# One core, two decoder blocks: the mixer's head norms, gates and last cell step placed in the memory stage, and output products that wait for the split parts one at a time

## What is computed

```python
go = rmsnorm(go.transpose(0, 2, 1, 3), gdn_norm_w) * jax.nn.silu(g_z...)
...
h = num / jnp.maximum(jnp.abs(den), jnp.exp(-m_t))[..., None]
...
mh = rmsnorm(mh.transpose(0, 2, 1, 3), mlstm_norm_w...) * jax.nn.sigmoid(m_o...)
mixed = jnp.concatenate([go..., mh...], axis=-1)
return mixed @ w_out
```

## Time and profile before

| | us |
|---|---|
| median of 3 runs | 2404.67 |
| lowest and highest | 2404.33, 2405.97 |
| span of the profiled execution | 2405.3 |
| PE busy in it | 2268.6 |
| DVE busy | 1544.9 |
| ACT busy | 1126.1 |
| POOL busy | 51.6 |

### The profile page before, as it was taken

How to read it: one execution, slowest core, us unless ns; L and a number is a source line. 1 busy time by engine, 2 the same in 40 slices (tenths; PEclk the granted TensorE clock), 3 DMA queues, 4 the chain that set the end, 5 groups by cost and what they waited for, 6 DMA issues and landing times. The chain is left out here.

```text
span 2405.3 us, 38363 instructions
## 1 busy us (share of the span) xinstructions
PE 2268.6 (94%) x15466; PEld 2086.1 (87%) x15466; DVE 1544.9 (64%) x2713; ACT 1126.1 (47%) x1961; POOL 51.6 (2%) x26
## 2 busy tenths in 40 slices
PE   8979888999999999999999999999999999988998
PEld 8867676999999997888878998979998899867997
DVE  7866445999888985666655456665456545575554
ACT  5523334455554445555555344444443434474443
POOL 0121000100000000000000000000000000000000
PEclk9989889999999999999999999999999999889999
DMA  6362233355444445666646555535555655303552
GB/s 260 139 67 91 88 129 127 120 178 182 158 142 148 144 147 177 193 195 194 195 127 251 182 187 211 193 134 215 191 178 192 228 183 186 125 19 123 197 188 105
DMA packets 78310, 390.25 MB, mean 162 GB/s; under 512 B 9772, under 2 KB 12716, under 8 KB 49741
## 3 DMA queue, kind: packets, MB, share of 16 engines
q1 hardware_dynamic: 76684, 383.59, 46.3%
q0 software_dynamic: 1040, 4.19, 1.6%
q10 hardware_dynamic: 432, 0.33, 0.0%
HBM read 382.83 MB, written 5.24 MB: 161 GB/s over the span
## 5 line engine op out<-in xcount | busy, mean ns | idle before, releaser
L246 DVE TENSOR_TENSOR split_slots<-ring,split_slots 128x1024 fp32r<-128x1024 f32 x406 | 481.9, 1232 | 333.7 <-ACT split_slots L237 333.6
L339 PE MATMUL banks<-x_transposed_hi,split_slots 128*128 128x256 f32 x1920 | 549.8, 286 | 8.8 <-DVE split_slots L246 5.2
L340 PE MATMUL banks<-x_transposed_lo,split_slots 128*128 128x256 f32 x1920 | 547.9, 285 | 0.0
L341 PE MATMUL banks<-x_transposed_hi,split_slots 128*128 128x256 f32 x1920 | 547.6, 285 | 0.0
L237 ACT ACTIVATE split_slots<-ring 128x1024 fp32r<-128x1024 f32 x406 | 404.4, 1049 | 222.6 <-PE banks L341 197.2
L350 DVE SCALAR_TENSOR_TENSOR expert_lo<-ring,expert_hi 128x512 fp32r<-128x512 f32 x512 | 363.2, 714 | 173.8 <-ACT expert_hi L345 172.7
L345 ACT ACTIVATE expert_hi<-ring 128x512 fp32r<-128x512 f32 x512 | 323.2, 632 | 266.8 <-PE banks L341 266.7
L339 PEld LDWEIGHTS banks<-x_transposed_hi,split_slots 128*128 128x128 f32 x1920 | 372.2, 194 | 11.5 <-DVE split_slots L246 5.6
L340 PEld LDWEIGHTS banks<-x_transposed_lo,split_slots 128*128 128x128 f32 x1920 | 372.1, 194 | 1.5
L341 PEld LDWEIGHTS banks<-x_transposed_hi,split_slots 128*128 128x128 f32 x1920 | 372.1, 194 | 0.0
L339 PE MATMUL banks<-x_transposed_hi,expert_hi 128*128 128x256 f32 x1024 | 296.8, 290 | 5.5 <-DVE expert_lo L350 5.5
(11 more groups left out here) (463 smaller groups left out, 3431.8 us busy)
## 6 DMA issues: line engine op xcount, KB each, us to landing
ring<-in_ffn_w SPq DMA_DIRECT2D x132, 1024.0 KB, 4.8
ring<-in_peer_u SPq DMA_DIRECT2D x128, 512.0 KB, 3.5
ring<-in_peer_v SPq DMA_DIRECT2D x128, 512.0 KB, 4.3
ring<-in_w_in SPq DMA_DIRECT2D x16, 1024.0 KB, 5.1
ring<-in_sgu_w_in SPq DMA_DIRECT2D x16, 1024.0 KB, 4.8
ring<-in_peer_wq SPq DMA_DIRECT2D x8, 1024.0 KB, 5.0
ring<-in_sgu_w_out SPq DMA_DIRECT2D x8, 1024.0 KB, 4.8
ring<-in_kv_w SPq DMA_DIRECT2D x6, 1024.0 KB, 4.8
```

The costliest lines, as they stand in the source:

```text
L246: ins = dve.tensor_tensor(self.parts[:, b, 1, p], self.k.w.slot(g)[:, p], self.parts[:, b, 0, p].bitcast(F32), ALU.subtract)
L339: pe.matmul(out, lh, rh, start=start, stop=False)
L340: pe.matmul(out, lh, rl, start=False, stop=False)
L341: return pe.matmul(out, ll, rh, start=False, stop=stop)
```

## The change

In the memory stage PE runs `memory_cell(3)` between the two halves of panel 6. ACT and DVE get the head norms and the gates there: squares, sums, roots, inverses, and the multiplications by scale and gate, in place in `s.go` and `s.mh`; the division by the denominators is there too. The mixer's output stage keeps the transposes (straight from `s.go` and `s.mh`, into banks 4 to 7), both halves of `Beginning`, and the splits of the four banks. `attend_memory` mixes into banks 4 to 7 as well. The output products don't wait for all parts at their head; before each tile of a slot PE waits for the count of written parts that the tile needs (`Before.part`). The tile `mixed` is gone.

```diff
@@ -296,8 +296,10 @@
 class Before:
 
 
-    def __init__(self, splits_eaten, highed=None, written=None, banks_read=()):
+    def __init__(self, splits_eaten, highed=None, written=None, banks_read=(), parts=None):
         self.splits_eaten, self.highed, self.written, self.banks_read = splits_eaten, highed, written, banks_read
+        self.parts = parts
+        self.waited = 0
 
     def rows_high(self, pe):
         for signal, value in self.banks_read:
@@ -308,6 +310,16 @@
     def rows_low(self, pe):
         if self.written:
             pe.wait_ge(*self.written)
+
+    def part(self, pe, m, i):
+
+        if m == 0 and i == 0:
+            for signal, value in self.banks_read:
+                pe.wait_ge(signal, value)
+        value = self.parts(m, i)
+        if value > self.waited:
+            self.waited = value
+            pe.wait_ge(self.written[0], value)
 
 
 def high_first(pe, before, out, operands, x_on_right):
...
@@ -1349,7 +1361,10 @@
         gain = k.sb(ctx, "head_gains", [P, HD + GW])
         vs, ps, acts, pools, landed, gained, panel_done, panel_read = (k.sig.new() for _ in range(8))
         ws, outs, dstate, mouts, mdstate, vns, decayed, gds, mds, rd, mrd = (k.sig.new() for _ in range(11))
-        A_, MAXD, MPREV, MNEXT, INTER, MT, SCARG, WARG, R, WGT = range(10)
+        head_squared, head_summed, head_rooted, head_inverted, head_scaled, divided = (k.sig.new() for _ in range(6))
+        A_, MAXD, MPREV, MNEXT, INTER, MT, SCARG, WARG, R, WGT, DEN = range(11)
+        SUMS, ROOTS, SCALES = 11, 13, 15
+        read, squares, gates = (s.go, s.mh), (diag, work), (s.z, s.mo)
         gl = s.glast[:, 0, :].rearrange("p (h n) -> p h n", h=HEADS)
         dec = s.glast[:, 1, :].rearrange("p (h n) -> p h n", h=HEADS)
 
@@ -1473,10 +1488,10 @@
             panel(5, 1)
             memory_cell(2)
             panel(6, 0)
+            memory_cell(3)
             panel(6, 1)
             panel(7, 0)
             panel(7, 1)
-            memory_cell(3)
 
         @block.vector
         def _(dve):
@@ -1594,6 +1609,43 @@
             low(7)
             mlstm_add(2)
 
+            def head_sums(n):
+                dve.wait_ge(head_squared, n + 1)
+                dve.tensor_reduce(c[:, SUMS + n, :], squares[n][:, :, :], AX_X, ALU.add).then_inc(head_summed, 1)
+
+            def scale_and_gate(n):
+                dve.wait_ge(head_rooted, n + 1)
+                dve.reciprocal(c[:, SCALES + n, :], c[:, ROOTS + n, :]).then_inc(head_inverted, 1)
+                dve.wait_ge(head_inverted, n + 1)
+                dve.wait_ge(gained, n + 1)
+                for i in range(TILES):
+                    own = read[n][:, i, :, :]
+                    dve.tensor_tensor(own, own, over_last(c[:, SCALES + n, HEADS * i:HEADS * i + HEADS], HD), ALU.mult
+                                      ).then_inc(head_scaled, 1)
+                    dve.wait_ge(head_scaled, TILES * n + i + 1)
+                    dve.tensor_tensor(own, own, gates[n][:, i, :].rearrange("p (h d) -> p h d", h=HEADS), ALU.mult)
+
+            def divide():
+                dve.wait_ge(mrd, NCHUNK)
+                by_tile = c[:, DEN, :].rearrange("p (i h) -> p i h", h=HEADS)
+                dve.scalar_tensor_tensor(by_tile, s.mden[:, :, :, 0], -1.0, s.mden[:, :, :, 0], ALU.mult, ALU.max
+                                         ).then_inc(divided, 1)
+                dve.wait_ge(divided, 1)
+                dve.tensor_tensor(by_tile, by_tile, s.emt[:, :].rearrange("p (h i) -> p i h", h=HEADS), ALU.max
+                                  ).then_inc(divided, 1)
+                dve.wait_ge(divided, 2)
+                dve.reciprocal(c[:, DEN, :], c[:, DEN, :]).then_inc(divided, 1)
+                dve.wait_ge(divided, 3)
+                dve.tensor_tensor(s.mh[:, :, :, :], s.mh[:, :, :, :],
+                                  over_last(c[:, DEN, :], HD).rearrange("p (i h) d -> p i h d", h=HEADS), ALU.mult
+                                  ).then_inc(divided, 1)
+
+            head_sums(0)
+            scale_and_gate(0)
+            divide()
+            head_sums(1)
+            scale_and_gate(1)
+
         @block.scalar
         def _(act):
             def delta_out(n):
@@ -1640,9 +1692,27 @@
             copy(5)
             split.high(act, 7)
             cell_out(2)
+
+            def head_squares(n):
+                act.activation(squares[n][:, :, :].rearrange("p (i h) d -> p i h d", h=HEADS), read[n][:, :, :, :], ACT.Square
+                               ).then_inc(head_squared, 1)
+
+            def head_roots(n):
+                act.wait_ge(head_summed, n + 1)
+                act.activation(c[:, ROOTS + n, :], c[:, SUMS + n, :], ACT.Sqrt, bias=k.eps[:, 0:1], scale=1.0 / HD
+                               ).then_inc(head_rooted, 1)
+
+            act.wait_ge(rd, NCHUNK)
+            act.wait_ge(ps, 3)
+            head_squares(0)
+            head_roots(0)
+            cell_out(3)
+            act.wait_ge(vs, 33)
+            act.wait_ge(divided, 4)
+            head_squares(1)
             copy(6)
+            head_roots(1)
             copy(7)
-            cell_out(3)
 
         @block.gpsimd
         def _(pool):
...
-        highs, lows = split_turned(k, 0, dst, banks, high, written)
+        highs, lows = split_turned(k, 4, dst, banks, high, written)
...
@@ -1687,46 +1745,24 @@
 
         @block.scalar
         def _(act):
-            act.activation(sq_g, s.go[:, :, :, :], ACT.Square).then_inc(acts, 1)
-            begin.high(act, 0)
-            act.wait_ge(vs, 4)
-            act.activation(sq_m, heads(mo), ACT.Square).then_inc(acts, 1)
-            act.wait_ge(vs, 6)
-            act.activation(c[:, 2, :], c[:, 1, :], ACT.Sqrt, bias=k.eps[:, 0:1], scale=1.0 / HD).then_inc(acts, 1)
-            begin.high(act, 1)
+            begin.highs(act)
             highs(act)
 
         @block.vector
         def _(dve):
-            link = linker(dve, vs)
-            d = c[:, 0, 0:8].rearrange("p (i h) -> p i h", h=HEADS)
-            link(dve.scalar_tensor_tensor(d, s.mden[:, :, :, 0], -1.0, s.mden[:, :, :, 0], ALU.mult, ALU.max))
-            link(dve.tensor_tensor(d, d, s.emt[:, :].rearrange("p (h i) -> p i h", h=HEADS), ALU.max))
-            link(dve.reciprocal(c[:, 0, 0:8], c[:, 0, 0:8]))
-            link(dve.tensor_tensor(heads(mo), src_m, per_head(c[:, 0, 0:8]), ALU.mult))
-            dve.wait_ge(acts, 1)
-            link(dve.tensor_reduce(c[:, 1, 0:8], sq[:, 0:8, :], AX_X, ALU.add))
-            begin.low(dve, 0)
-            dve.wait_ge(acts, 2)
-            link(dve.tensor_reduce(c[:, 1, 8:16], sq[:, 8:16, :], AX_X, ALU.add))
-            dve.wait_ge(acts, 3)
-            link(dve.reciprocal(c[:, 3, :], c[:, 2, :]))
-            for i in range(TILES):
-                for n, (src, out, gate) in enumerate(((s.go, go, s.z), (heads(mo), mo, s.mo))):
-                    own = heads(out)[:, i, :, :]
-                    scale = over_last(c[:, 3, 8 * n + 4 * i:8 * n + 4 * i + 4], HD)
-                    link(dve.tensor_tensor(own, src[:, i, :, :], scale, ALU.mult))
-                    dve.tensor_tensor(out[:, i, :], out[:, i, :], gate[:, i, :], ALU.mult).then_inc(normed, 1)
-            begin.low(dve, 1)
+            begin.lows(dve)
             lows(dve)
 
         @block.tensor
         def _(pe):
             for i in range(TILES):
-                turn_chunks(pe, k, mixed[:, i, :], i, banks, 0, normed)
+                for n, heads in enumerate((s.go, s.mh)):
+                    for h in range(HEADS):
+                        ins = pe.transpose(k.psum[:, 4 + 2 * i + n, h * P:(h + 1) * P], heads[:, i, h, :], k.ident[:, :])
+                    ins.then_inc(banks, 1)
 
         k.idle_pool(block)
-        k.before = Before((written, 4), (high, 4), (written, 4))
+        k.before = Before((written, 4), (high, 4), (written, 4), parts=lambda m, i: 2 * i + m // 2 + 1)
     return gains_landed, 32
 
 
...
@@ -1796,7 +1832,7 @@
         c = k.sb(ctx, "xa_columns", [P, 4, PAIRS])
         scored, maxed, negated, expd, recip, scaled, turned, copied, mixed, high, written = (k.sig.new() for _ in range(11))
 
-        highs, lows = split_banks(k, 0, k.xT, mixed, high, written)
+        highs, lows = split_banks(k, 4, k.xT, mixed, high, written)
         begin, before = Beginning(k), k.before
 
         @block.sync
@@ -1825,7 +1861,7 @@
                 for half in range(2):
                     for m in range(2):
                         lo = h * DH + half * P
-                        ins = pe.matmul(k.psum[:, h, half * SEQ:(half + 1) * SEQ], v[:, m, lo:lo + P],
+                        ins = pe.matmul(k.psum[:, 4 + h, half * SEQ:(half + 1) * SEQ], v[:, m, lo:lo + P],
                                         probT[:, h, m, :], start=(m == 0), stop=(m == 1))
                 ins.then_inc(mixed, 1)
 
@@ -1860,7 +1896,7 @@
             highs(act)
 
         k.idle_pool(block)
-        k.before = Before((written, 4), (high, 4), (written, 4))
```

(15 more changed lines are left out.)

14 lines of the change are left out of this document (1 added, 13 removed).

## The result

The changed kernel takes 2385.7 us (median of 4 runs, 2384.55 to 2390.2), the kernel before 2404.5 beside it: 18.8 us faster. The ratio is 0.9924, with a 95% interval from 0.9912 to 0.9937, which is 15 to 21 us. The forecast was 2389.0, 15.7 us faster. The profiled execution of the changed kernel is the one that took 2390.2 us, the highest of its four, with a span of 2388.4; against the profiled span of before that is 16.9 us. A run's time is 1.8 to 1.9 us longer than the span of the same execution. So the profiled execution of before, with its span of 2405.3, took about 2407.1 and lies some 2.5 us above its median, and not between the lowest and the highest run; that of the changed kernel lies 4.5 above its own. The difference is why the two spans show 16.9 and the medians 18.8.

A forecast was written before the change was run, and what follows sets the result against it. PE was taken to bound the kernel, busy 2268.6 of 2405.3 us; 11.3 + 1.9 + 1.4 + 1.1 = 15.7 us gave span 2389.6, and with the median 0.6 below it, 2389.0. Range 2385.5 to 2394.

The forecast's parts named there:

- The memory stage: Moved cell and head work fit beside PE's last panels: cost 0, DVE ending at 283.3 with 1 us to spare.
- The seam: Between memory stage and mixer's output products: PE starts its products at 288.7 instead of 299.96, 11.3 us sooner.
- The clock: The 96 products behind the mixer run at full clock, 22.47 us instead of 24.39: 1.9 us won.
- a fall in the seam: Rival: the clock falls ahead of the mixer's output products, gain 13.8 us, 2390.9; chance 0.25, including the skill's rule.
- The rival from the Trainium skill's rule: Transposes don't count as busy time, so the clock is gone at the mixer's output: 2390.9; chance 0.05 of the 0.25.
- The two attentions: PE's waits before output products shrink: 1.4 us won behind the cross attention, 1.1 behind the sparse attention.
- the waits by parts bring nothing: Rival: at both attentions another wait takes their place, gain 13.2 us, 2391.5; chance 0.08.
- the chain doesn't fit: Rival: DVE's moved chain outlasts the panels and holds the memory stage's end, 2390.5 to 2393; chance 0.12.
- the head work runs late: Rival: memory-stage head work runs behind PE's last product, costing 7.6 us, 2396.6, or 2402.2 if delta is late; chance 0.05.
- the cell stalls PE: Rival: the last cell stalls PE in panel 6 because DVE's state comes late; 2409 with 20 us; chance 0.02.
- each later stop of PE meets the clock in another phase: Behind the change, each stop may move up to 1.9 us either way; 3 us allowed in the sum.

The follow-up runs named there:

- three kernels with delays: Changed kernel with 14, 22 or 34 more products ending PE's memory-stage work, about 1.0, 2.0 and 3.4 us of delay: 2388.13, 2390.21 and 2388.48 us.
- whole waits: Changed kernel, but PE waits for all written parts in front of each of the three output products, as before: 2396.13 us.
- the long transposes: Changed kernel with 80 more transposes behind the sixteen of the mixer's output stage: 2390.91 us in one run.
- the second median: The changed kernel measured again with no edit: 2385.33 us, 5 runs, ratio 0.9920.
- the run with the longer chain: Changed kernel with three more sums, results not used, in DVE's chain for the mLSTM half: 2389.59 us in one run.

## Why the prediction was right

It was right in direction, size and mechanism, 3 us short in the total, and the reason that it gave for the clock in the seam was too weak.

**The memory stage.** DVE's chain was put at 283.3 with 1 us to spare before the stage's end. It ended at 284.07 in an execution that was 0.6 late, 283.5, with 0.9 to spare. The stage's end was to be unmoved; it came 0.15 later. That the cell's wait costs nothing held. DVE was not busy all the time, as I had said it would be: it waits 1.22 us for the last cell, 1.19 for ACT's squares and twice 0.37 for a root.

**The seam.** 11.3 was forecast, 30.71 - 19.59 = 11.1 measured; the missing 0.15 is the stage's end. Slot 1 was to be ready 0.4 us ahead of PE. The first two of DVE's six low parts from 292.27 are slot 1's; at 6.91 us for six they were ready at 292.27 + 2.3 = 294.6, and PE was through slot 0, a quarter of the 22.48, at 289.44 + 5.6 = 295.0.

**The clock.** 1.9 was forecast, 24.39 - 22.48 = 1.91 measured. The rival, a fall in the seam, did not come in either trace of the changed kernel. The reason that was given does not carry this, though. The prediction counted the clock as kept because each gap was shorter than the 2.7 us in which it had fallen; with gaps of 0.30 and 2.24 us, no longer than those of the changed kernel, it fell in two of the three kernels with delays, for 1.5 and 1.4 us. With whole waits and 4.03 us idle it fell too. So the term was right and in part lucky, and the chance of 0.25 for a fall was not too high. The rival from the Trainium skill's rule fell with the long transposes.

**The two attentions.** 1.4 and 1.1 were forecast; both waits, 1.46 and 1.15, are gone.

**The rivals.** That the waits by parts bring nothing is refuted by the run without them. That the chain doesn't fit, that the head work runs late and that the cell stalls PE are refuted by the rows: panels 6 and 7 follow the cell without a gap. The run with the cell last gives the price that "late head work" would have had, 7.5 us for my sum of 7.6, and the clock with it, which that rival left out.

**What was off.** The total. The places of the change hold 15.7 us, and the medians 18.6 to 18.8. At 2385.7 us the result lies 0.2 inside the low end of the range, 2385.5, and the second median, 2385.33, lies 0.2 outside it. The step that was too small is "each later stop of PE meets the clock in another phase": I took it as noise around the sum, 3 us either way. Over 129 runs of all kernels of this study (each less the mean of its kernel) the time goes with the mean granted clock, -1.2 us for each 0.001 of clock, with a correlation of -0.73. The changed kernel's runs have 0.970, those of before 0.965 in the middle. In the traces the changed kernel has fewer stretches at a lowered clock: that at 890 us is at full clock in both executions, those at 1255 and 1450 in the second alone. In these traces, then, what lies beyond the sum is clock. That it is so for the medians is likely and not shown, since the one trace of the kernel before is not of an execution at its median. And that the shift of 13 to 16 us brings it, and would bring it again, is not shown at all. The delayed kernels show in their rows that the clock at one stop can be there or gone after a pure shift, for 1.5 us; what sets it at the stops far behind stays open.

## What to carry to other kernels

Work that runs alone at a stage's end may be done beside the last products if the step that feeds it is put one place earlier in PE's list; add up the chain on the other engines behind that step and compare it with what PE still has to do, and the difference is the spare time. A wait in front of products should name the part that the first product reads: it is worth its own length, and more where the shorter idle time keeps the clock up. Read a change of some us off the rows at its own places, not off the total: 1.1 us that were plain in the rows did not show in five runs, and the clock at stops far behind moved the total by 4.

## What the runs showed of the hardware

- Ahead of the mixer's output products PE stands still twice, with 1.94 us of transposes between. With 0.94 and 2.24 us the clock stayed full in both traces of the changed kernel; with 0.30 and 2.24 it fell in two kernels of three; with 0.94 and 1.10 it stayed, with 0.94 and 4.03 it fell, and so it did with 3.42 ahead of the transposes. So the same 2.24 us of idle time did one or the other.
- Ninety-six fp32 transposes in a row held it at 1.00. In the run with the longer chain it rose from 0.50 to 1.00 behind 3.2 us in which PE ran transposes alone.
- The same kernel, with the same distances to the hundredth around the change, took 2383.5 and 2388.4 us of span; 3.5 of the 4.9 us lie between the two attentions, where two stretches had the clock at 0.50 to 0.54 in one and at 1.00 in the other, about 1.7 us each.
- A pure delay of 2.0 us on PE cost 3.4 us up to the end of the 96 products behind it, and one of 3.4 us cost 3.4 too, as the clock fell in the first and not in the second. In the kernel before, the median with 26 added products rose by 5.3 us and that with 34 by 3.5; the intervals overlap.
- Three sums of 128x1024 in a row on DVE took 3.39 us, where one alone took 1.21 or 1.22.
